# Outset of a two-block transformer kernel in column halves, with three chunks of the modulation loaded and summed elsewhere

## The chip, the cores and the metric

The kernel runs on one NeuronCore of a Trainium2 chip. The metric is the device time of one execution in microseconds (us). TensorE, VectorE, ScalarE, GpSimdE and SyncE are called PE, DVE, ACT, POOL and SP, as the profile does.

## The reference

One sequence of 512 tokens with 1024 features goes through two blocks. Only the first branch of the first block is touched here.

```python
cond = jax.nn.silu(c)
mod = cond @ w_ada[l] + b_ada[l]                     # 1024 -> 9 x 1024
sh1, sc1, gt1, sh2, sc2, gt2, sh3, sc3, gt3 = split(mod, 9)
u = rmsnorm(h, g_norm_ffn1) * (1 + sc1) + sh1
h = h + 0.5 * gt1 * swiglu(u, w_ffn1_in, w_ffn1_out) # 1024 -> 2 x 2816 -> 1024
...                                                  # token mixing, second feed-forward network,
                                                     # second block with two mixture-of-experts layers
```

## The kernel before

Activations lie feature-major: eight tiles k of 128 features by 512 tokens. A weight chunk is 1 MB, 128 partitions by 2048 numbers. Most matrix products are made of float32 numbers split in two: ACT copies a chunk or tile to a rounded high part (`weights_high`, L845; `tile_high`, L848), DVE subtracts to get the low part (`weights_low`, L1361; `tile_low`, L1367), and PE runs three matmuls of 128x512 for each tile (`passes`, L2193). A product over eight tiles is 24 matmuls.

**Stream.** SP loads all chunks of the first block in one fixed order (`stream_a`, issued at L600) into a ring of six slots (`slot_a`; slot n % 6 at the outset). Before each load it waits for the semaphore value that frees the slot; a load that waits holds all later ones back. The order at the outset is two chunks of the modulation matrix `w_ada`, x, six more chunks of `w_ada`, the two chunks of the first pair of the feed-forward network, three later chunks of `w_ada`, the second pair, two of `w_ada`, and so on. The first eight chunks (`ADA_FIRST`) hold scale and shift of the first norm, 256 rows by 1024 columns each (rows of 4 KB in memory); all other weight chunks of this stage are 1024 rows by 256 columns (1 KB). Chunks of the output matrix have 512 columns (2 KB).

**Outset.** PE multiplies the first two chunks by silu(c) (`ada_rows`, L2135), transposes x (L2178), takes two more chunks, spreads the reciprocal roots over the partitions (`rstd`, L2160), sums the scale (`ada_sums`, L2145), takes four chunks for the shift and sums it (L2145). ACT squares x (L829), evicts the eight transposed tiles to H (`evac`, L823) and then computes the root (L882, L886). DVE makes the reciprocals and a diagonal (`roots`, L1395, L1397), copies the scale rows (L1617), multiplies H by gain and reciprocal root (`normed`, L1631) and, when the shift is there, makes low parts of the tiles (L1638) while ACT makes high parts (L902). Only then does PE begin the first pair.

**Pairs.** The first projection of the network runs in 11 pairs, c = 0 to 10; a pair is four products, which = 0 or 1 (the silu side, `ffn_a`, and the other, `ffn_b`) for s = 0 or 1, into banks 2s + which. The first product starts the next as soon as DVE has multiplied the two results of a bank pair (`tile`, L1428, which signals `ffn_g`). In the gaps DVE adds up later chunks of `w_ada` weighted by silu(c) (`ada`, L1322 to L1335, one call for each chunk): three in pair 0, two in pairs 1 to 9, three in pair 10.

**Output projection.** `outproj` takes twelve chunks; chunk q needs the low part of its weights and, one by one, the low parts of its four tiles. DVE makes them in `out_low`, in this order for each q: whatever `idle` holds for q, then the chunk's low part, then four tiles:

```python
if q in idle:
    idle[q]()
...
if q:
    weights_low(split_at[name] + q)
    ...
            tile_low(m, pair, out_slot(name, q) + k - k0, rhs(k))
```

Before, `idle` holds `angles` for q = 2 and `modulation` for q = 4. The first four tiles of chunk 0 are made ahead, in pair 10.

Of the kernel before, what the change touches and what calls it, by code (L numbers as in the profile page):

```python
# [7 lines left out]
F32 = mybir.dt.float32  # L8
# [7 lines left out]
P = 128  # L16
# [113 lines left out]
def build(nc, A, out):  # L130
    with ExitStack() as ctx:
# [247 lines left out]
        def ffn_at(i, c):  # L379

            if i:
                return first["ffn1"] + 2 * c + (LATE_HERE if c else 0)
            return first["ffn0"] + (0 if c == 0 else 5 + 4 * (c - 1))

        def ada_of(c):

            a = ADA_FIRST + (0 if c == 0 else 3 + 2 * (c - 1))
            return list(range(a, a + (3 if c in (0, 10) else 2)))
# [14 lines left out]
        ada_first = tuple(range(ADA_FIRST))  # L403
# [58 lines left out]
        def slot_a(n):  # L462

            if n < first["mix"]:
                return n % RING
# [33 lines left out]
        for name, which, ns in [  # L499
                ("ffn0", "a", [ffn_at(0, c) + w for c in range(FT // 2) for w in range(2)]),  # L500
                ("ffn0_out", "a", range(first["ffn0_out"], first["ffn0_out"] + 12)),
# [314 lines left out]
        def _(act):  # L816
# [60 lines left out]
            def norm(i, shift, split=False):  # L877

                if i == 0:
                    act.wait_ge(sem("pool_step"), 4)  # L880
                    st.wait()
                A_(small[:, 56:57], epsc[:, 0:1], ACT.Sqrt)  # L882
                if i:
                    squares(i, range(4, KT))
                    act.wait_ge(sem("sumsq"), i)
# [4 lines left out]
                if i == 0:  # L890
                    act.wait_ge(sem("ada_mm"), 8)
                    act.wait_ge(sem("ada_mod"), 4)
                    for h in range(2):
                        evac(AROW[:, h], bank[4 + h][:], "ada_row")
                    weights_high(0)
                    act.wait_ge(sem("ada_mod"), ADA_FIRST)
                for k in range(KT):
                    if i == 0 and k == 2:
                        weights_high(1)
# [8 lines left out]
                if i == 1:  # L908
                    act.wait_ge(sem("u"), KT)
                    tile_high(UM[0][:, KT - 1], U[:, KT - 1])  # L910

            def ffn(i):
# [11 lines left out]
                weights_high(s0 + 3)  # L924
                with act.Fori(0, 3) as it:
# [185 lines left out]


            norm(0, lambda k: mod[:, k:k + 1], True)
            act.wait_ge(sem("side_tp"), 1)
            evac(LROW[0:64], bank[7][0:64, 64:64 + P], "side_out")
# [182 lines left out]
        def _(dve):  # L1298
# [122 lines left out]
            def ffn(i):  # L1421
# [8 lines left out]
                def some_ada(c, it, which):  # L1430

                    for m in which:
                        a = ada_of(c)[m]
                        now = a if it is None else it * 6 + a
                        ada(ffn_at(0, c) + 2 + m, now, a, 0 if it is None else it * 32)
# [6 lines left out]

                def pair(c, it, s_next):


                    n = 3 if c in (0, 10) else 2
# [21 lines left out]
                def modulation():  # L1468
                    if i:
# [15 lines left out]
                        {4: modulation} if i else {2: angles, 4: modulation}, staged=True)  # L1485
# [125 lines left out]
            nc.vector.tensor_copy(CZ[:, :, 0:1], csil[:].unsqueeze(2)).then_inc(sem("ada_cz"), 1)  # L1611

            def vector(v):
                if v == 0:
                    dve.wait_ge(sem("ada_mm"), 4)
                    for h in range(2):
                        nc.vector.tensor_copy(AROW[:, h], bank[4 + h][:]).then_inc(sem("ada_row"), 1)  # L1617
                dve.wait_ge(sem("ada_sum"), v + 1)
                c = KT * (1 - v)
                TTn(mod[:, c:c + KT], bank[7][:, 16 * v:16 * v + KT], par[:, PC["b_ada"] + c:PC["b_ada"] + c + KT], ALU.add)\  # L1620
                    .then_inc(sem("ada_mod"), 4)

            dve.wait_ge(sem("keep"), 16)
            roots(0)
            vector(0)
            dve.wait_ge(sem("ada_mod"), 4)
            modulated_gains(0)
            dve.wait_ge(sem("rstd"), 1)
            st.wait()
            for k in range(KT):  # L1630
                STT(out=U[:, k], in0=H[:, k], scalar=gains[:, k:k + 1], in1=bank[6][:],  # L1631
                    op0=ALU.mult, op1=ALU.mult).then_inc(sem("normed"), 1)
            vector(1)
            weights_low(0)
            dve.wait_ge(sem("ada_mod"), ADA_FIRST)
            for k in range(KT):
# [3 lines left out]
            weights_low(1)  # L1640
# [473 lines left out]
        def _(pe):  # L2114
# [11 lines left out]
            def ada_rows(a):  # L2126

                landed(pe, "a", ada_first[a])
                if a == 4:
                    pe.wait_ge(sem("ada_row"), 2)  # L2130
                w = chunk("a", ada_first[a])
                for half in range(2):
                    for k in range(2):
                        at = 32 * ((2 * half + 2 * a + k) % 4)
                        x = mm(bank[4 + half][at:at + 32, :], CZ[:, 2 * (a % 4) + k], w[:, k, 512 * half:512 * half + 512],  # L2135
                               start=(a % 4 < 2), stop=(a % 4 > 1))
                x.then_inc(sem("ada_mm"), 1)

            def ada_sums(v):

                for half in range(2):
                    pe.wait_ge(sem("ada_row"), 2 * v + half + 1)
                    for q in range(4):
                        c = 16 * v + 4 * half + q
                        x = mm(bank[7][:, c:c + 1], AROW[:, half, P * q:P * q + P], ones[:, 0:1], start=True, stop=True)  # L2145
                x.then_inc(sem("ada_sum"), 1)
# [22 lines left out]
            pe.wait_ge(sem("ada_cz"), 1)  # L2169
            ada_rows(0)  # L2170
            ada_rows(1)
            pe.wait_ge(sem("x_in"), 16)
# [10 lines left out]
            tp(bank[7][0:64, 64:64 + P], par[:, PC["ln1_g"]:PC["ln1_g"] + 64], ident).then_inc(sem("side_tp"), 1)  # L2183
            ada_sums(0)
            for a in range(4, ADA_FIRST):
                ada_rows(a)
# [9 lines left out]

            def ffn(i):
                a, b, g, base, s0 = sem("ffn_a"), sem("ffn_b"), sem("ffn_g"), FT * i, split_at[f"ffn{i}"]

                def pair(c, r, it):  # L2200

                    for s in range(2):
# [3 lines left out]
                        if s == 0 and it is None and r == 0 and i:  # L2206
                            pe.wait_ge(sem("w_low"), s0 + 2)
                        if it is None and r == s == 0:
                            tiles = [(which, k) for which in range(2) for k in range(KT)]
                            for which, k in sorted(tiles, key=lambda v: v[1]) if i else tiles:  # L2210
                                if i == 0 and k == 0:
                                    pe.wait_ge(sem("w_low"), s0 + which + 1)
# [14 lines left out]
                pair(0, 0, None)  # L2227
# [617 lines left out]
```

## Time and profile before

| | us |
|---|---|
| median of three runs (lowest, highest) | 2662.53 (2661.29, 2663.78) |
| profiled execution | 2662.51 |
| its span in the trace | 2660.5 |
| PE busy in the span | 2420.2 |

The trace starts with the first instruction. Each row of a timeline gives its start and its length in us, engine, line, operation, what it writes and reads, its shape and the number of instructions in the row; in brackets stands the idle time of the engine before it and what ended that.

### The profile page before, as it was taken

The page shows a single profiled execution, that of the slowest core. Times are in us where ns is not written, and L with a number is a line of the kernel's source. Part 1 is how long each engine was busy: PE and PEld are TensorE (multiplying, and loading weights), DVE is VectorE, ACT ScalarE, POOL GpSimd, SP SyncE. Part 2 cuts the span into 40 slices and gives each one's busy share as a digit, 9 for nine tenths or more (in the row PEclk, how much of TensorE's full clock was granted, in tenths as well). Part 3 has the DMA queues.
Part 4 walks back from the last instruction along what each step waited for, and adds up shares of the span by engine and source line. Part 5 has one row for each costly group of instructions (what it writes and reads, how often), then busy time and mean ns, then how long its engine had stood idle before and what let it go on. Part 6 is the DMA issues. An engine that isn't in the chain of part 4 may idle for free.

```text
span 2660.5 us, 38185 instructions
## 1 busy us (share of the span) xinstructions
PE 2420.2 (91%) x14539; PEld 1778.2 (67%) x14540; DVE 1353.0 (51%) x2767; ACT 860.4 (32%) x1484; POOL 215.5 (8%) x168
## 2 busy tenths in 40 slices
PE   6999999999999999999987887889989988888787
PEld 4888888877678888788754444547755865544454
DVE  5766645443552244543753444336955574344445
ACT  4222335565232223322322111124367341221122
POOL 1000003000000000000011111110036001111110
PEclk9999999999999999999999898899999999899899
DMA  8666422212333233221499999995220359999987
GB/s 287 213 196 196 166 87 86 67 48 80 131 110 102 100 103 102 96 95 64 180 386 422 422 422 422 422 401 196 80 95 19 149 196 422 422 422 422 422 339 306
DMA packets 201771, 591.62 MB, mean 222 GB/s; under 512 B 10512, under 2 KB 126432, under 8 KB 152784
## 3 DMA queue, kind: packets, MB, share of 16 engines
q1 hardware_dynamic: 198496, 575.47, 56.2%
q0 software_dynamic: 2896, 14.47, 1.7%
q8 instruction: 61, 1.00, 0.2%
q10 hardware_dynamic: 288, 0.43, 0.1%
q14 instruction: 30, 0.25, 0.0%
HBM read 588.17 MB, written 7.41 MB: 224 GB/s over the span
## 4 chain that ended last, share of the span: by engine, by line
PE 68%; DMA 21%; DVE 4%; ACT 3%; issue 2%; SPq 1%; POOL 1%; DVEq 0%; ACTq 0%; POOLq 0%
PE bank L2193 42%; DMA arena<-in_exp_w 19%; PE bank L2566 7%; PE bank L2287 4%; PE bank L2589 1%; SPq L611 1%; PE bank L2454 1%; PE bank L2607 1%; PE bank L2801 1%; PE bank L2377 1%; DVE ring_low L1361 1%; DMA ring<-in_exp_w 1%; PE bank L2535 1%; PE bank L2770 1%; PE bank L2536 1%
## 5 line engine op out<-in xcount | busy, mean ns | idle before, releaser
L2193 PE MATMUL bank<-parts 128*128 128x512 f32 x2560 | 795.4, 392 | 10.1 <-DVE parts L1638 4.3
L2193 PEld LDWEIGHTS bank<-parts 128*128 128x128 f32 x2560 | 482.1, 189 | 111.7 <-issue 6.5
L2193 PE MATMUL bank<-parts,ring_low 128*128 128x512 f32 x1280 | 500.3, 391 | 0.0
L2566 PE MATMUL bank<-ring,arena 128*32 128x256 f32 x2112 | 301.8, 445 | 84.6 <-DMA arena<-in_exp_w 84.4
L1361 DVE TENSOR_TENSOR ring_low<-ring,parts 128x2048 fp32r<-128x2048 f32 x109 | 245.1, 2252 | 177.8 <-ACT parts L845 168.6
L2566 PE MATMUL bank<-arena 128*32 128x256 f32 x2112 | 302.0, 445 | 33.2 <-issue 24.8
L845 ACT ACTIVATE parts<-ring 128x2048 fp32r<-128x2048 f32 x109 | 204.5, 1879 | 222.4 <-DMA ring<-in_w_ffn_in 114.4
L2193 PEld LDWEIGHTS bank<-parts,ring_low 128*128 128x128 f32 x1280 | 241.6, 189 | 51.1
L772 POOL COPY arena<-U 128x2048 f32<-128x2048 f32 x60 | 112.6, 1908 | 1756.0 <-PE bank L2566 1038.4
L2566 PEld LDWEIGHTS bank<-ring,arena 128*32 128x32 f32 x2112 | 141.6, 123 | 156.7 <-issue 132.6
L2566 PEld LDWEIGHTS bank<-arena 128*32 128x32 f32 x2112 | 144.5, 123 | 82.1 <-issue 50.0
L2193 PE MATMUL bank<-ring_low 128*128 128x512 f32 x576 | 194.1, 396 | 1.8 <-ACT arena L1157 1.8
L1077 ACT ACTIVATE arena<-bank 128x128 f32<-128x128 f32 x66 | 18.3, 278 | 537.3 <-PE bank L2566 537.3
L2607 PE MATMUL bank<-parts 128*128 128x512 f32 x496 | 129.8, 403 | 27.7 <-DVE parts L1924 26.8
L1919 DVE TENSOR_TENSOR arena<-bank,arena 128x128 f32<-128x128 f32 x66 | 19.2, 291 | 256.6 <-ACT arena L1077 256.6
L1940 DVE TENSOR_TENSOR H<-bank,H 128x512 f32<-128x512 f32 x232 | 143.8, 683 | 6.5 <-PE bank L2607 6.5
L2607 PEld LDWEIGHTS bank<-parts 128*128 128x128 f32 x496 | 87.2, 188 | 84.9 <-DVE parts L1924 40.2
L823 ACT ACTIVATE arena<-bank 128x512 f32<-128x512 f32 (+2 forms) x171 | 73.0, 467 | 209.4 <-PE bank L2536 95.4
L848 ACT ACTIVATE parts<-arena 128x512 fp32r<-128x512 f32 x128 | 71.4, 621 | 195.6 <-PE bank L2193 129.5
L1367 DVE TENSOR_TENSOR parts<-arena,parts 128x512 fp32r<-128x512 f32 x128 | 80.8, 687 | 105.5 <-ACT parts L848 105.2
L2193 PEld LDWEIGHTS bank<-ring_low 128*128 128x128 f32 x576 | 108.3, 188 | 31.0 <-issue 5.4
L2287 PE MATMUL bank<-parts 128*128 128x512 f32 x384 | 122.0, 395 | 3.9 <-DVE parts L1367 3.1
(380 smaller groups left out, 3584.1 us busy)
## 6 DMA issues: line engine op xcount, KB each, us to landing
ring<-in_exp_w SPq DMA_DIRECT2D x188, 1024.0 KB, 19.7
arena<-in_exp_w SPq DMA_DIRECT2D x132, 1024.0 KB, 18.6
U<-in_exp_w SPq DMA_DIRECT2D x60, 1024.0 KB, 23.1
ring<-in_w_ffn_in SPq DMA_DIRECT2D x44, 1024.0 KB, 5.6
ring<-in_w_ada SPq DMA_DIRECT2D x36, 1024.0 KB, 5.2
ring<-in_w_ffn_out SPq DMA_DIRECT2D x20, 1024.0 KB, 5.0
ring<-in_w_in SPq DMA_DIRECT2D x18, 1024.0 KB, 5.0
ring<-in_conv_w_in SPq DMA_DIRECT2D x12, 1024.0 KB, 5.1
```

Of the source, the lines that this page charges most:

```text
L611: sp.dma_start(dst, rows_of(layer, j, e)).then_inc(sem(f"w_e{3 * i + j}"), 16)
L772: pool.tensor_copy(W13[0][:, j], AHEAD[:, j]).then_inc(sem(f"w_e{j}"), 16)
L823: A_(dst, src, ACT.Copy).then_inc(sem(s), 1)
L845: A_(buf, ring[:, slots[which][n], 0:nk * cols], ACT.Copy).then_inc(sem("w_high"), 1)
L848: A_(dst, src, ACT.Copy).then_inc(sem("t_high"), 1)
L1361: TTn(ring_low[:, n, 0:nk * cols], ring[:, n, 0:nk * cols], buf.bitcast(F32), ALU.subtract)\
L1367: TTn(pair[1][:, at], src, pair[0][:, at].bitcast(F32), ALU.subtract).then_inc(sem("t_low"), 1)
L1940: x = TTn(H_, bank[sum_bank(t, h)][:], H_, ALU.add)
L2193: i = mm(o, a[:, cols[0], cols[1]], b, start=first_ and n == 0, stop=last_ and n == 2)
L2287: last = mm(bank[4 * half + t][:], a[:, at, P * t:P * t + P], b[:, k - 4 * c, :], start=(k == m == 0), stop=(k == kts - 1 and m == 2))
L2566: x = mm(bank[p][lanes_at:lanes_at + LANES, 0:2 * P].rearrange("p (w n) -> p w n", w=2), XW[:, k, LANES * (2 * p + e):LANES * (2 * p + e) ...
L2607: x = mm(bank[at][:], OHT[:, P * t:P * t + P], part[:, h], start=(j == 0), stop=(j == 1))
```

## The change

The outset works in column halves. The first eight chunks of `w_ada` become four rows of tiles by 512 columns (2 KB rows), ordered scale half 0, shift half 0, scale half 1, shift half 1; only four of them lie ahead of the first pair's weights, the other four behind. The slots of the first 15 loads are listed by hand. DVE, not ACT, evicts the transposed x to H. When four tiles of the normed input are done, PE multiplies them with the half chunks (`first_pair`), and between products makes the modulation of the other half. Pair 0 keeps one late chunk for DVE after its two tiles; two chunks move from it to the output projection, loaded as its third and fourth load and added up by DVE at q = 1. The transpose of the layer-norm parameters and its eviction move behind pair 0.

```diff
-            return first["ffn0"] + (0 if c == 0 else 5 + 4 * (c - 1))
+            return first["ffn0"] + (0 if c == 0 else 6 if c == 1 else 3 + 4 * c)
...
+                    if name == "ffn0_out" and n == 3:
+                        ada_chunks(2)
...
-                    stream_a.append((flat(A["w_ada"], 2 * (a % 4), 2, D * (1 - a // 4), D), 2, D, "ada_mm", a + 1))
+                    stream_a.append((flat(A["w_ada"], 4 * (a % 2), 4, D * (1 - a // 2 % 2) + 512 * (a // 4), 512), 4, 512,
+                                     "ada_mm", a + 1))
...
-        ada_chunks(ADA_FIRST)
+        ada_chunks(4)
...
-                    ada_chunks(3 if c in (0, 10) else 2)
+                    ada_chunks({0: 4, 1: 3, 10: 3}.get(c, 2))
...
+            if n < ffn_at(0, 2):
+                return (5, 0, 3, 4, 1, 2, 5, 0, 3, 4, 5, 0, 3, 1, 2)[n]
...
-            for k in range(KT):
-                act.wait_ge(sem("x_tp"), k + 1)
-                evac(H[:, k], bank[k % 4][:], "x_h")
...
+            def first_norm():
...
+                row(1)
+                first_high(0, 0)
+                act.wait_ge(sem("ada_mod"), 4)
+                tile(0)
+                tile(1)
+                first_high(1, 0)
+                tile(2)
+                tile(3)
+                first_high(0, 1)
+                first_high(1, 1)
+                row(2)
+                row(3)
+                act.wait_ge(sem("ada_mod"), ADA_FIRST)
+                for k in range(4, KT):
+                    tile(k)
...
+                def two_ada():
+
+                    for m in range(2):
+                        ada(first["ffn0_out"] + 2 + m, ADA_FFN - 2 + m, ADA_FFN - 2 + m)
...
+                    if i == 0 and c == 0:
+                        for s in s_next:
+                            weights_low(s)
+                        tile(0, 0)
+                        tile(1, 1)
+                        some_ada(0, None, range(1))
+                        return
...
-                        {4: modulation} if i else {2: angles, 4: modulation}, staged=True)
+                        {4: modulation} if i else {1: two_ada, 2: angles, 4: modulation}, staged=True)
...
+            dve.wait_ge(sem("ada_mm"), 2)
+            nc.vector.tensor_copy(AROW[:, 0], bank[4][:]).then_inc(sem("ada_row"), 1)
+            vector(0)
+            for k in range(KT):
+                dve.wait_ge(sem("x_tp"), k + 1)
+                nc.vector.tensor_copy(H[:, k], bank[k % 4][:]).then_inc(sem("x_h"), 1)
+                if k == 6:
+                    dve.wait_ge(sem("keep"), 16)
+                    roots(0)
+            dve.wait_ge(sem("x_h"), KT)
+            dve.wait_ge(sem("rstd"), 1)
+            normed(0)
+            vector(1)
+            first_low(0, 0)
+            rest_of(0)
+            normed(1)
+            rest_of(1)
+            normed(2)
+            first_low(1, 0)
+            rest_of(2)
+            normed(3)
+            rest_of(3)
+            first_low(0, 1)
+            first_low(1, 1)
+            vector(2)
+            for k in range(4, KT):
+                normed(k)
+            vector(3)
+            for k in range(4, KT):
+                rest_of(k)
...
+            def first_pair():
...
+                pe.wait_ge(sem("opening"), 2)
+                for k in range(4):
+                    pe.wait_ge(sem("t_low"), tiles_at["ffn0"] + k + 1)
+                    for s in range(2):
+                        product(0, s, k)
+                ada_rows(4)
+                ada_rows(5)
+                pe.wait_ge(sem("opening"), 3)
+                for k in range(4):
+                    product(1, 0, k)
+                    if k == 1:
+                        ada_sums(2)
+                ada_rows(6)
+                ada_rows(7)
+                for k in range(4):
+                    product(1, 1, k)
+                    if k == 1:
+                        ada_sums(3)
+                pe.wait_ge(sem("w_low"), 2)
+                for which in range(2):
+                    for k in range(4, KT):
+                        pe.wait_ge(sem("t_low"), tiles_at["ffn0"] + k + 1)
+                        for s in range(2):
+                            x = product(which, s, k)
+                            if k == KT - 1:
+                                x.then_inc(sem(("ffn_a", "ffn_b")[which]), 1)
```

## Rows read from the trace of the kernel before

**Rows 1.** The chain that ended last, 110 to 420 us: start, length, what, count.

```profile
109.93 195.52 PE bank L2193 x861
```

**Rows 2.** Waits of PE, 40 to 420 us: total us, times, longest.

```profile
PE bank L2193 <- DVE ring_low L1361: 0.7, 1, 0.7
```

**Rows 3.** Timeline of PE at the outset: start, length, line, shape, count [idle before].

```profile
16.71 3.67 PE L2178 MATMUL bank<-keep,arena 128*128 128x128 f32 x16 [3.19 <-DMA arena<-in_x]
21.49 2.11 PE L2178 MATMUL bank<-keep,arena 128*128 128x128 f32 x16 [1.11 <-ACT H L823]
...
30.26 3.64 PE L2135 MATMUL bank<-ring,arena 128*32 128x512 f32 x32
34.63 1.95 PE L2145 MATMUL bank<-ones,arena 128*128 128x1 f32 x16 [0.73 <-ACT arena L823]
40.92 1.19 PE L2193 MATMUL bank<-parts 128*128 128x512 f32 x2 [4.34 <-DVE parts L1638]
```

**Rows 4.** Timeline of ACT at the outset, and one half chunk later.

```profile
20.87 3.98 ACT L823 ACTIVATE H<-bank 128x512 f32<-128x512 f32 x8
...
26.26 0.28 ACT L886 ACTIVATE small<-small,epsc 128x4 f32<-128x4 f32 x1
...
40.72 3.77 ACT L902 ACTIVATE parts<-U,mod 128x512 fp32r<-128x512 f32 x6
...
318.99 1.05 ACT L845 ACTIVATE parts<-ring 128x1024 fp32r<-128x1024 f32 x1
```

**Rows 5.** Timeline of DVE at the outset, and one half chunk later.

```profile
27.65 1.28 DVE L1617 COPY arena<-bank 128x512 f32<-128x512 f32 x2
...
30.93 5.35 DVE L1631 SCALAR_TENSOR_TENSOR U<-H,gains,bank 128x512 f32<-128x512 f32 x8
...
37.81 2.29 DVE L1361 TENSOR_TENSOR ring_low<-ring,parts 128x2048 fp32r<-128x2048 f32 x1 [0.96 <-ACT parts L845]
...
320.06 1.23 DVE L1361 TENSOR_TENSOR ring_low<-ring,parts 128x1024 fp32r<-128x1024 f32 x1
```

**Rows 6.** Busy time by stretch: engines in turn, then clock, DMA share, GB/s.

```profile
10.00:20.00 10.00, 5.22 (x24) 3.47 (x24) 0.00 (x0) 3.31 (x7) 0.00 (x0) 1.00 1.02 414
30.00:40.00 10.00, 5.85 (x51) 3.04 (x51) 8.04 (x12) 5.21 (x6) 0.00 (x0) 0.89 1.08 352
285.00:290.00 5.00, 5.00 (x23) 3.99 (x22) 4.79 (x12) 3.32 (x5) 0.00 (x0) 1.00 1.01 379
40.92:44.66 3.74, 3.74 (x9) 2.97 (x10) 3.72 (x6) 3.73 (x7) 0.00 (x0) 0.50 1.10 347
```

**Rows 7.** Timeline of SP, the loads that the end of pair 0 frees.

```profile
64.75 1.00 SPq L600 DMA_DIRECT2D ring<-in_w_ada  x2
```

**Rows 8.** Timeline of DVE from pair 10 into the output projection.

```profile
274.48 2.29 DVE L1361 TENSOR_TENSOR ring_low<-ring,parts 128x2048 fp32r<-128x2048 f32 x1 [7.34 <-ACT parts L845]
...
279.69 0.61 DVE L1322 TENSOR_SCALAR arena<-ring,csil 128x256 f32<-128x256 f32 x2
...
289.24 0.68 DVE L1428 TENSOR_TENSOR arena<-bank,arena 128x512 f32<-128x512 f32 x1
...
292.04 2.49 DVE L1367 TENSOR_TENSOR parts<-arena,parts 128x512 fp32r<-128x512 f32 x4
...
303.19 2.49 DVE L1367 TENSOR_TENSOR parts<-arena,parts 128x512 fp32r<-128x512 f32 x4
```

**Rows 9.** Timeline of ACT, the tiles that wait for PE's first output chunk.

```profile
294.57 2.19 ACT L848 ACTIVATE parts<-arena 128x512 fp32r<-128x512 f32 x4 [4.05 <-PE bank L2193]
```

**Rows 10.** The page's DMA issues: KB each, median us from issue to landing.

```profile
ring<-in_w_ada SPq DMA_DIRECT2D x36, 1024.0 KB, 5.2
```

**Rows 11.** Timeline of PE, a later wait.

```profile
532.62 2.10 PE L2394 MATMUL bank<-arena 64*128 64x512 f32 x4 [2.13 <-ACT arena L1153]
```

**Rows 12.** Busy time of PE by stretch, then its clock, after two waits.

```profile
532.78:536.17 3.39, 3.39 (x14) 0.50 0.03 7
...
1508.99:1515.79 6.80, 5.85 (x56) 0.50 1.02 424
```

More of the change, by code:

```diff
@@ L402, in build @@
         first["ada"] = 0
-        ada_first = tuple(range(ADA_FIRST))
+        ada_first = tuple(a if a < 4 else a + 2 for a in range(ADA_FIRST))
         def ada_chunks(n):
@@ L500, in build @@
                 ("ffn0", "a", [ffn_at(0, c) + w for c in range(FT // 2) for w in range(2)]),
[L501 removed]
+                ("ffn0_out", "a", [first["ffn0_out"] + q + (2 if q > 1 else 0) for q in range(12)]),
                 ("mix", "a", [mix_at[c] for c in (0, 1, 2, 3, 4, 5, 6, 8, 9)]),
@@ L910, in norm, with first_high, row, tile @@
                     tile_high(UM[0][:, KT - 1], U[:, KT - 1])
+            def first_high(i, part):
+                which, n = splits[i]
+                landed(act, which, n)
+                C = slice(CHUNK // 2 * part, CHUNK // 2 * part + CHUNK // 2)
+                made = A_(high(i)[0][:, C], ring[:, slots[which][n], C], ACT.Copy)
+                if part == 0:
+                    st.did(made)
+                else:
+                    made.then_inc(sem("w_high"), 1)
+            def first_norm():
+                act.wait_ge(sem("pool_step"), 4)
+                st.wait()
+                A_(small[:, 56:57], epsc[:, 0:1], ACT.Sqrt)
+                A_(small[:, 48:52], small[:, 60:64], ACT.Sqrt, scale=1.0 / D, bias=epsc[:, 0:1]).then_inc(sem("root"), 1)
+                def row(g):
+                    act.wait_ge(sem("ada_mm"), 2 * g + 2)
+                    if g >= 2:
+                        act.wait_ge(sem("ada_sum"), g - 1)
+                    evac(AROW[:, g % 2], bank[4 + g % 2][:], "ada_row")
+                def tile(k):
+                    act.wait_ge(sem("normed"), k + 1)
+                    A_(UP[0][:, k], U[:, k], ACT.Identity, bias=mod[:, k:k + 1]).then_inc(sem("t_high"), 1)
+                row(1)
[13 more added lines that the diff above has]
+                    tile(k)
             def ffn(i):
@@ L1623, in _, with vector @@
[L1623 to L1630, printed above, removed]
+            nc.vector.tensor_copy(CZ[:, :, 0:1], csil[:].unsqueeze(2)).then_inc(sem("opening"), 1)
+            def vector(g):
+                dve.wait_ge(sem("ada_sum"), g + 1)
+                c = KT * (1 - g % 2) + 4 * (g // 2)
+                TTn(mod[:, c:c + 4], bank[7][:, 4 * g:4 * g + 4], par[:, PC["b_ada"] + c:PC["b_ada"] + c + 4], ALU.add)\
+                    .then_inc(sem("ada_mod"), 2)
+                dve.wait_ge(sem("ada_mod"), 2 * g + 2)
+                if g % 2 == 0:
+                    C = slice(2 * g, 2 * g + 4)
+                    seq(STT(out=gains[:, C], in0=mod[:, c:c + 4], scalar=1.0, in1=par[:, PC["g_ffn1"] + 2 * g:PC["g_ffn1"] + 2 * g + 4],
+                            op0=ALU.add, op1=ALU.mult))
@@ L1631, in _, with first_low, normed @@
+            def first_low(i, part):
+                dve.wait_ge(*((sem("act_step"), TT + i + 1), (sem("w_high"), i + 1))[part])
+                n = slots["a"][splits[i][1]]
+                C = slice(CHUNK // 2 * part, CHUNK // 2 * part + CHUNK // 2)
+                TTn(ring_low[:, n, C], ring[:, n, C], high(i)[0][:, C].bitcast(F32), ALU.subtract)\
+                    .then_inc(sem(("opening", "w_low")[part]), 1)
+            def normed(k):
                 STT(out=U[:, k], in0=H[:, k], scalar=gains[:, k:k + 1], in1=bank[6][:],
@@ L1632, in _, with rest_of @@
                     op0=ALU.mult, op1=ALU.mult).then_inc(sem("normed"), 1)
[L1633 to L1636, printed above, removed]
+            def rest_of(k):
                 dve.wait_ge(sem("t_high"), tiles_at["ffn0"] + k + 1)
@@ L2205, in pair @@
                             pe.wait_ge(g, c * 2 + (base + s - 1))
-                        if s == 0 and it is None and r == 0 and i:
+                        if s == 0 and it is None and r == 0:
                             pe.wait_ge(sem("w_low"), s0 + 2)
                         if it is None and r == s == 0:
[L2209 to L2212, printed above, removed]
+                            for which, k in [(which, k) for k in range(KT) for which in range(2)]:
                                 pe.wait_ge(sem("t_low"), tiles_at[f"ffn{i}"] + k + 1)
```

85 lines of the change are left out of this document (33 added, 52 removed).

## The prediction

> **What bounds the kernel now.** I read the chain that ended last first. From 110 to 305 us it is one row of matmuls, 861 in 195.52 us, 0.227 us each [rows 1]: in the first stage PE never waits, so time counts only where PE is idle, runs at the lower clock or gets extra work. The waits of PE confirm it: between 40 and 420 us there are two waits for the first projection's operands, 4.34 us ahead of the first pair [rows 3] and 0.7 us in the third pair [rows 2]. Then the timelines: of PE, ACT and DVE at the outset, to see what the first pair waits for; and of DVE where the output projection begins, because the change puts work there. Last the stretches with the clock. Two places matter:
>
> The outset. x is there at 16.7 us, but the first pair starts at 40.92 [rows 3], and the loads that its end frees go out at 64.75 [rows 7]; so pair 0 ends at 64.75. Of these 23.8 us, 96 matmuls at 0.227 are 21.8. Most of the rest is the clock: from 40.92 to 44.66 it is at 0.50, 1.2 GHz, after an engine that had waited 4.34 us, and 9 matmuls start where 16.5 would have [rows 6], a loss of 7.5 x 0.227 = 1.7 us.
>
> The start of the output projection. PE ends its first chunk at 294.5 (ACT's tiles that wait for this start at 294.57 [rows 9]). The second chunk needs a tile that DVE begins at 292.04; four take 2.49 [rows 8], so the first is there at 292.7. DVE is 1.8 us ahead, no more, and it has no idle time from 276.7 on: it comes out of two late chunks (279.69 to 289.24, 9.55 us for both [rows 8]).
>
> **The change, part by part.** Durations come from the profiled execution, 2662.51 us, which is the median of the three runs to 0.02; so the sum is made against 2662.5.
>
> 1. Loads ahead of x. The two chunks now have rows of 2 KB, not 4. Loads ran at 414 GB/s where rows were 4 KB and 379 where output chunks with 2 KB rows dominate [rows 6]: 1.049 MB takes 2.77 in place of 2.53 us, so x lands 0.5 us later, at 17.2. The Trainium skill's page "DMA: Bandwidth & Descriptors" (Why small descriptors are slow) tells of a fixed overhead of about 3 cycles for a packet beside one cycle for 32 bytes, which would make 2 KB rows 2.3% dearer than 4 KB rows: 0.1 us for both chunks, and a total 0.4 us lower. The rows are nearer to this case, and I keep them. Behind x come two chunks (2.77 each), then the pair's weights at 352 GB/s [rows 6], 2.98 each: 25.7 and 28.7, where the first of them used to land at 35.9. The other four chunks follow by 40, ahead of their use.
>
> 2. Eviction of x moves from ACT to DVE. ACT needs 3.98 us for eight and could not start before 20.87, because it squares x [rows 4]; a DVE copy of this size costs 1.28 for two [rows 5], 0.6 in sequence. The skill's page "VectorE: DVE Perf Modes" (its first table, Memory placement) has ScalarE closer to PSUM, which speaks against the move; the rows agree in sign, 0.1 us a tile, and by that alone 0.8 us would be lost. But DVE is free from the first transposed tile on. Transposes take 3.67 + 2.11 us without the 1.11 us in which PE waited for an eviction [rows 3]: 17.2 to 23.0. The root no longer stands behind 3.98 us of evictions: 26.26 - 3.98 + 0.5 = 22.8 [rows 4]. From there to the end of DVE's root work took 1.39 us (26.26 to 27.65 [rows 4, 5]): 24.2; the last eviction ends at 24.8. PE's two chunks at 0.91 (3.64 for four) and the spreading of the roots, eight instructions at 0.13 (2.11 for 16) [rows 3], end at 25.9. The first normed tile starts there, where it started at 30.93 [rows 5].
>
> 3. The ladder of four tiles. On DVE: eight tile operations at 0.67 (5.35 for eight), two half weights at 1.23 [rows 5], 0.2 for the shift, and two waits for ACT's high part, 0.63 [rows 4] and hand-over 0.1 each, the other two being covered by the half weights. Sum 5.4 + 2.5 + 0.2 + 1.5 = 9.6, so the fourth tile's low part is there at 35.5, and with 0.15 to PE at 35.7. Halving costs 2 x 1.23 - 2.29 = 0.17 us a chunk on DVE, hidden for the later halves. PE's two products for a tile are 1.36 us, less than the ladder's 2.4 a tile.
>
> 4. PE from there: the last tile, 1.36, to 37.1; then four chunks of the other half (3.64), two groups of sums (1.95) [rows 3] and 24 matmuls (5.45): 48.1. Their evictions by ACT lie beside the products that stand behind them. The last sum ends 1.36 earlier, at 46.8; shift, high and low part of tile 4 take 0.2 + 0.7 + 0.75 + 0.1, to 48.5: PE idles 0.4. Then 48 matmuls, 10.9, to 59.4. Both results of s = 0 now end almost together, so pair 1 waits for one DVE multiply: 59.7. The wait stands behind DVE's two `weights_low` of pair 1, which end at about 59. **Gain 64.75 - 59.7 = 5.0 us.**
>
> 5. The clock on this way. PE idles some 2 us before the ladder and is sparse on it; a wait of 2.13 us [rows 11] was followed by 3.39 us at 0.50 [rows 12], so I expect a low stretch here. A tile costs about 2.5 us then, as much as the ladder. Bounds: nothing, or a stretch like the longest shown, 5.85 us of work at 0.50 [rows 12], wholly on the dense part: 5.85 x 7.5/16.5 = 2.7. I take 0.4, since PE's work begins 8 us before the dense part does.
>
> 6. Pair 0 keeps one late chunk in place of three, behind its tiles, so DVE is not late in pairs 1 and 2; the 0.7 us wait [rows 2] goes. **Gain 0.7.** The parameters' transpose and its eviction moved behind pair 0 cost PE one short instruction. SP's loads for the late chunks of pair 1 now wait for pair 0 and hold pair 2's weights back, as a wait there did before; these are needed 20 us later, so I cost that at nothing; without the cover it would be one landing, 5.2 us [rows 10].
>
> 7. Two late chunks at q = 1. They stand on DVE ahead of the second output chunk's low part and its four tiles. Everything behind moves by 9.55: the first tile is there at 292.7 + 9.55 = 302.3 (on the clock of before), where PE is done at 294.5. **PE idles 7.8 us.** Their loads do not make it later: they go out when the last product of the projection ends, 48 x 0.23 = 11 us before 294.5, land in 5.2 us [rows 10], at 288.6, and DVE is not free until 289.8. Next late is the third chunk: its first tile was begun at 303.19 [rows 8], 11.15 us behind the second chunk's; PE needs 10.9 for a chunk, so nothing more is lost.
>
> 8. The clock behind that wait. A wait of this length is followed by a low stretch, of 3.39 to 5.85 us of work [rows 12]: 1.5 to 2.7 us; at least nothing. I take 2.0, near what pair 0 paid (1.7) [rows 6].
>
> Sum: -5.0 - 0.7 + 0.4 + 7.8 + 2.0 = +4.5, **2667.0 us**. With the bounds of 5 and 8: 2662.5 - 5.7 + 7.8 = 2664.6 to 2662.5 - 5.7 + 2.7 + 7.8 + 2.7 = 2670.0.
>
> **The rivals.**
>
> A, not slower: DVE reaches q = 1 earlier, so the two chunks are covered. For: it idles 7.34 us ahead of 274.48 [rows 8], and pair 10 could start sooner. Against: that idle time is a wait for ACT and so for the load of the first output chunk, which stands in the same order behind the same three late chunks and is freed by the same pair 9. It decides if DVE is 7.8 us earlier against PE; if all the idle time went, 0.5 us of wait is left, no low clock: 2662.5 - 5.3 + 0.5 = 2657.7.
>
> B, slower: the outset's low clock falls on the dense part after 37 us, not on the ladder. For: PE is sparse until then, and pair 0 was at 0.50 for its first 3.74 us [rows 6]. Against: at 0.50 the ladder itself keeps PE busy. It decides if the clock is still low at 37: 2.3 us more, 2669.3; with the longer low stretch in the output projection 2670.0.
>
> C, the change does not do what it says: first products at 28 us still wait on something I miss on ACT (a row eviction behind its half chunks) and pair 0 ends at 62, a gain of 2.7 in place of 5: 2669.3. Nothing in the rows shows it.
>
> **How the numbers follow.** Forecast 0.57, A 0.13, B 0.17, C 0.13. About 0.2%, 5.3 us, is what a measurement of this kernel can tell from no change, so faster means under 2657.2, slower over 2667.8. A lies just inside; with half its spread beyond, and a remainder from the forecast's mechanism being wrong altogether, faster 0.09. The forecast's own range, 2664.6 to 2670, has about a quarter of its chance above 2667.8 (0.14); with B and C nearly whole, slower is 0.41, same 0.50. Range: A's 0.13 and 0.05 above are left out: 2661.5 to 2671.
>
> **What would show it.** In the changed profile: the first matmul of the pair at about 29 us, DVE's first normed tile at 26, pair 0 ending near 59.5, no wait near 90 us; in the output projection a wait of PE near 8 us for DVE's tile low parts (L1367's successor), its weights' low part directly behind ten operations of two late chunks, and the clock at 0.50 behind it. Wrong would be a wait there under 3 us (then A), or pair 0 ending after 61 (then B or C, told apart by the clock after 37 us).

## The result and the profile after

| | before | after |
|---|---|---|
| median of 15 runs each, us | 2662.53 | 2667.43 |
| lowest to highest, us | 2658.68 to 2667.40 | 2664.58 to 2670.25 |
| profiled execution, us | 2662.51 | 2666.85 |
| its span, us | 2660.5 | 2665.0 |

The ratio after to before is 1.0017, with a 95% interval of 1.0010 to 1.0024: 4.9 us more, and 4.3 more between the two profiled executions. That is inside the 0.2% within which the prediction speaks of no change, but the interval leaves out 1: the kernel became a little slower, although its first pair ends 4.8 us earlier. Where the gain went is to be read in four places. All medians here and below are of fast executions; the slow ones, all over 3000 us (one of the kernel before in the later runs, one of e4_act_evicts, two of e7_busy_outset), are left out.

**PE at the outset and in the output projection**, timeline of the kernel after: start, length, line, shape, count [idle before, and what ended it].

```profile
16.71 5.65 PE L2258 MATMUL bank<-keep,arena 128*128 128x128 f32 x32 [0.52 <-DMA arena<-in_x]
28.43 1.19 PE L2269 MATMUL bank<-parts 128*128 128x512 f32 x2 [2.34 <-DVE parts L1689]
36.88 1.92 PE L2214 MATMUL bank<-ring,arena 128*32 128x512 f32 x16
48.91 0.70 PE L2269 MATMUL bank<-parts 128*128 128x512 f32 x2 [0.53 <-DVE parts L1689]
59.92 0.27 PE L2305 MATMUL bank<-keep,par 128*64 128x128 f32 x1
60.34 0.73 PE L2269 MATMUL bank<-parts 128*128 128x512 f32 x2
...
297.19 1.19 PE L2269 MATMUL bank<-parts 128*128 128x512 f32 x2 [7.74 <-DVE parts L1405]
```

L2269 is the product line (L2193 in [rows 3]), L1689 the low part of a tile at the outset (L1638), L1405 the low part of a tile of the output projection (L1367). x is there at 16.71, to the hundredth as in [rows 3]. The first product stands at 28.43 where it stood at 40.92, but it is the start of a ladder that DVE paces; the dense work begins at 36.88. Pair 0 ends at 59.92 and pair 1 starts at 60.34, where pair 0 ended and pair 1 began at 64.75. From there the chain that ended last is again one row of matmuls:

```profile
60.34 196.16 PE bank L2269 x864
```

864 matmuls in 196.16 us are 0.227 each, the step of [rows 1]: a lead won ahead of this row is carried through it unchanged. The first chunk of the output projection ends at 297.19 - 7.74 = 289.45, against 294.5 before: 5.05 us ahead. Then PE waits 7.74 us, and the lead is gone.

**The waits of PE** from 40 to 420 us in the kernel after: in total, times, longest.

```profile
PE bank L2269 <- DVE parts L1405: 7.7, 1, 7.7
PE bank L2463 <- ACT U L897: 1.7, 1, 1.7
PE bank L2239 <- DVE diag L1435: 0.9, 1, 0.9
PE bank L2269 <- DVE parts L1689: 0.5, 1, 0.5
```

The 0.7 us of [rows 2] in the third pair is no longer there; the 7.7 is new. **DVE around it**, timeline:

```profile
269.28 2.29 DVE L1399 TENSOR_TENSOR ring_low<-ring,parts 128x2048 fp32r<-128x2048 f32 x1 [7.23 <-ACT parts L851]
...
284.63 0.61 DVE L1360 TENSOR_SCALAR arena<-ring,csil 128x256 f32<-128x256 f32 x2
289.49 0.62 DVE L1360 TENSOR_SCALAR arena<-ring,csil 128x256 f32<-128x256 f32 x2
294.16 2.28 DVE L1399 TENSOR_TENSOR ring_low<-ring,parts 128x2048 fp32r<-128x2048 f32 x1
296.36 2.49 DVE L1405 TENSOR_TENSOR parts<-arena,parts 128x512 fp32r<-128x512 f32 x4
```

L1360 is the first operation of a late chunk (L1322 in [rows 8]), L1399 the low part of a weight chunk (L1361). The two late chunks that q = 1 got stand from 284.63 to 294.16, 9.5 us, ahead of the low part of the second chunk's weights. PE runs out of operands at 289.45, when DVE is between the first of them and the second. **The clock behind the wait**, busy time by stretch (PE, weight loads, DVE, ACT, POOL, each with its instructions; then granted clock, DMA share, GB/s):

```profile
293.80:297.15 3.35, 0.00 (x0) 0.00 (x0) 3.33 (x4) 1.72 (x1) 0.00 (x0) 0.50 0.05 18
297.19:300.60 3.41, 3.41 (x8) 2.73 (x9) 3.31 (x7) 0.00 (x0) 0.00 (x0) 0.50 0.00 0
300.65:310.00 9.35, 9.35 (x49) 7.43 (x47) 9.10 (x14) 0.00 (x1) 0.00 (x0) 1.00 0.01 2
```

The granted clock falls to 0.50 (1.2 GHz) while PE waits, and stays there for the first 3.41 us of work: 8 matmuls start in it, where the step of 0.227 us would make it 15, so 7 x 0.227 = 1.6 us are lost. The sum from these rows is -5.05 + 7.74 + 1.6 = +4.3 us, which is the difference of the profiled executions.

### The profile page after: what moved, and what is told of

The parts are those of the page before. It is cut to its first block, busy times and chain, and to the rows that moved or that the text cites. A ratio compares the mean times of both kernels' runs of the same rounds, so it can differ in the third digit from the quotient of the medians.

```text
span 2665.0 us, 38207 instructions
## 1 busy us (share of the span) xinstructions
PE 2427.1 (91%) x14539; PEld 1780.4 (67%) x14540; DVE 1358.2 (51%) x2779; ACT 857.9 (32%) x1479; POOL 215.5 (8%) x168
## 4 chain that ended last, share of the span: by engine, by line
PE 66%; DMA 22%; DVE 5%; issue 2%; ACT 2%; SPq 1%; POOL 1%; DVEq 0%; POOLq 0%
PE bank L2269 41%; DMA arena<-in_exp_w 19%; PE bank L2676 7%; PE bank L2397 4%; DMA ring<-in_exp_w 2%; PE bank L2699 1%; SPq L621 1%; PE bank L2564 1%; PE bank L2911 1%; DVE ring_low L1399 1%; PE bank L2487 1%; PE bank L2880 1%; PE bank L2717 1%; PE bank L2645 1%; PE bank L2646 1%
## 5 line engine op out<-in xcount | busy, mean ns | idle before, releaser
L2269 PE MATMUL bank<-parts 128*128 128x512 f32 x2560 | 798.2, 393 | 15.8 <-DVE parts L1405 7.7
L2269 PEld LDWEIGHTS bank<-parts 128*128 128x128 f32 x2560 | 482.9, 189 | 120.3 <-issue 9.6
L2269 PE MATMUL bank<-parts,ring_low 128*128 128x512 f32 x1280 | 501.3, 392 | 0.0
L1399 DVE TENSOR_TENSOR ring_low<-ring,parts 128x2048 fp32r<-128x2048 f32 x107 | 240.5, 2251 | 181.0 <-ACT parts L851 172.3
L2269 PEld LDWEIGHTS bank<-parts,ring_low 128*128 128x128 f32 x1280 | 242.5, 189 | 51.1
L2269 PE MATMUL bank<-ring_low 128*128 128x512 f32 x576 | 194.1, 396 | 1.8 <-ACT arena L1195 1.8
L833 ACT ACTIVATE arena<-bank 128x512 f32<-128x512 f32 (+3 forms) x172 | 73.7, 468 | 215.4 <-PE bank L2646 95.4
L1405 DVE TENSOR_TENSOR parts<-arena,parts 128x512 fp32r<-128x512 f32 x128 | 80.7, 686 | 104.1 <-ACT parts L854 103.8
L2269 PEld LDWEIGHTS bank<-ring_low 128*128 128x128 f32 x576 | 108.4, 188 | 30.9 <-issue 5.4
```

The source lines that it names most:

```text
L833: A_(dst, src, ACT.Copy).then_inc(sem(s), 1)
L1399: TTn(ring_low[:, n, 0:nk * cols], ring[:, n, 0:nk * cols], buf.bitcast(F32), ALU.subtract)\
L1405: TTn(pair[1][:, at], src, pair[0][:, at].bitcast(F32), ALU.subtract).then_inc(sem("t_low"), 1)
L2269: i = mm(o, a[:, cols[0], cols[1]], b, start=first_ and n == 0, stop=last_ and n == 2)
```

## Experiments

The theory: the wait at q = 1 is DVE's 9.5 us of two late chunks set against the lead of 1.8 us that DVE has there, and costs 7.7 us and the clock behind it; it has nothing to do with the new outset. The rivals: the wait came with the outset (PE reaches q = 1 sooner); the loads are late; or the outset gained less than the timeline suggests and something later gives it back.

Each ratio below is taken against executions of the kernel before that ran beside that kernel (median 2662.57 us beside e1, e2, e3 and e5, 2662.89 beside e4, e6 and e7). The intervals are about as wide as the effects, and most that one would compare overlap. The profiled executions are sharper. The chain that ended last holds, in all nine kernels, a row of 18 matmuls, 4.21 us long, near the end of the output projection. The last column counts to it from the start of pair 1 (with the old outset, from the loads that the end of pair 0 frees), so it leaves out the outset and all that stands behind the projection.

| kernel | pair 1 begins, us | row of 18 begins, us | between, us |
|---|---|---|---|
| before | 64.75 | 399.24 | 334.49 |
| after | 60.34 | 403.75 | 343.41 |
| e1_late_q4 | 60.19 | 394.00 | 333.81 |
| e2_out_alone | 64.36 | 407.08 | 342.72 |
| e3_one_q1 | 60.13 | 398.58 | 338.45 |
| e4_act_evicts | 64.30 | 407.88 | 343.58 |
| e5_kept_busy | 60.85 | 402.68 | 341.83 |
| e6_three_pair0 | 60.09 | 396.58 | 336.49 |
| e7_busy_outset | 60.82 | 394.64 | 333.82 |

**e1_late_q4: the two late chunks at another place.** The kernel after, with the work of the two chunks put three output chunks later. Their loads stay where they are, and so does all of the outset.

```diff
-                        {4: modulation} if i else {1: two_ada, 2: angles, 4: modulation}, staged=True)
+                        {4: modulation} if i else {2: angles, 4: two_ada, 5: modulation}, staged=True)
...
-                        if a1 and half == 0 and c == 2:
+                        if a1 and half == 0 and c == (4 if name == "ffn0_out" else 2):
```

> The changed kernel with its two late chunks added up at q = 4 of the output projection in place of q = 1; the fold of the sums on PE moves to the fifth output chunk and the modulation to q = 5. Loads and their order stay. Theory (the loss of the change is DVE's order at q = 1): DVE has some 9 us to spare before the fifth chunk's low parts are due, so the 7.7 us wait of PE and the low clock behind it (3.4 us of work at 1.2 GHz, 1.6 us lost) go: 2667.4 - 9.3 = 2658.1, and the wait at the second output chunk is gone from the profile. Rival (two more loads ahead of the third output chunk, or the ring's new slots, hold PE back wherever the sums stand): a wait of 3 us or more remains in the output projection, 2663 or more.

Measured: 2658.26 us, 0.9983 of before (0.9974 to 0.9992). The waits of its PE from 40 to 420 us, and a stretch with the first of the two chunks, which now stand from 304.85 to 314.39 us on DVE:

```profile
PE bank L2463 <- ACT U L897: 1.7, 1, 1.7
PE bank L2239 <- DVE diag L1435: 1.0, 1, 1.0
PE bank L2269 <- DVE parts L1689: 0.5, 1, 0.5
```

```profile
300.00:310.00 10.00, 10.00 (x45) 8.28 (x45) 9.68 (x19) 4.01 (x5) 0.00 (x0) 1.00 0.24 57
```

The wait is gone and no other has come in its place; DVE is busy for 9.68 of 10 us and PE for 10.00 of 10 beside it, at full clock. The difference to the kernel after is 9.2 us by the medians and 343.41 - 333.81 = 9.6 in the table, against 7.7 + 1.6 = 9.3 from the rows. This version is ahead of both kernels. It does not answer the question of the loads, since they have 20 us more to land here; the kernel after does: its DVE begins the multiply ahead of the chunks at 284.04, the first chunk at 284.63 and the second at 289.49, with no idle time before either, so it did not wait for the loads.

**e2_out_alone: the output projection's part alone.** The outset of before, with only the late chunks moved: pair 0 keeps one, two are loaded behind the first chunks of the output projection and added up at q = 1.

```diff
-            a = ADA_FIRST + (0 if c == 0 else 3 + 2 * (c - 1))
-            return list(range(a, a + (3 if c in (0, 10) else 2)))
+            a = ADA_FIRST + (0 if c == 0 else 1 + 2 * (c - 1))
+            return list(range(a, a + {0: 1, 10: 3}.get(c, 2)))
...
+                    if name == "ffn0_out" and n == 3:
+                        ada_chunks(2)
...
-                        {4: modulation} if i else {2: angles, 4: modulation}, staged=True)
+                        {4: modulation} if i else {1: two_ada, 2: angles, 4: modulation}, staged=True)
```

> The kernel before with only the late chunks moved: one in pair 0, two at q = 1 of the output projection with their loads third and fourth there. The outset is that of before. Theory: the same 7.8 us wait and low clock (1.6 to 2.0) as in the changed kernel, less the 0.7 us wait of the third pair, which goes: 2662.5 + 8.9 = 2671.4. Rival (the wait arises because the changed outset shifts DVE against PE): no wait or a short one, 2662 to 2665.

Measured: 2670.94 us, 1.0032 of before (1.0019 to 1.0044). The first two rows of its waits of PE, from 20 to 420 us (its L1369 is the low part of a tile of the output projection, its L1645 that of a tile at the outset), and the matmul behind the first of these waits:

```profile
PE bank L2200 <- DVE parts L1369: 7.7, 1, 7.7
PE bank L2200 <- DVE parts L1645: 4.5, 1, 4.5
```

```profile
300.80 1.19 PE L2200 MATMUL bank<-parts 128*128 128x512 f32 x2 [7.67 <-DVE parts L1369]
```

The same 7.7 us with PE 3.7 us later (it runs out of work at 300.80 - 7.67 = 293.13, against 289.45), and the outset's old wait (4.34 in [rows 3], 4.5 here) is still paid. So the wait belongs to the place q = 1: DVE's lead is a lead over PE, and an earlier outset moves both. It also prices the two halves of the change: the moved chunks cost 2670.9 - 2662.6 = 8.4 us by the medians and 342.72 - 334.49 = 8.2 in the table (7.7 + 1.6 less the 0.7 of the third pair would be 8.6). The new outset brings 2670.9 - 2667.4 = 3.5 by the medians, but the intervals of this kernel and of the kernel after overlap (1.0019 to 1.0024); in the profiles pair 1 begins 64.36 - 60.34 = 4.0 us earlier.

**e3_one_q1: one late chunk at q = 1, the other at q = 4.** The size of the cause is halved; `two_ada` takes the number of the chunk.

```diff
-                        {4: modulation} if i else {1: two_ada, 2: angles, 4: modulation}, staged=True)
+                        {4: modulation} if i else {1: lambda: two_ada(0), 2: angles, 4: lambda: two_ada(1), 5: modulation}, staged=True)
```

> Half the dose: one late chunk at q = 1, the other at q = 4. Theory: DVE is 1.8 us ahead there and a chunk costs 4.8, so PE waits 3.0 us, and the clock still falls: 2658.1 + 3.0 + 1.6 = 2662.7, 2661.1 if so short a wait leaves the clock alone. Rival (the wait is set by the landing of the two loads, not by DVE's work): the wait stays near 5 to 8 us, 2665 or more.

Measured: 2662.41 us, 0.9994 of before (0.9985 to 1.0003). Its wait at q = 1, from the waits of PE, and two stretches, the wait and what follows it; then the first and the last matmuls that start in the second stretch:

```profile
PE bank L2268 <- DVE parts L1405: 2.8, 1, 2.8
```

```profile
289.30:292.00 2.70, 0.00 (x0) 0.01 (x1) 2.70 (x3) 2.70 (x4) 0.00 (x0) 1.00 1.00 366
293.15:296.55 3.40, 3.40 (x10) 2.65 (x9) 3.23 (x7) 1.57 (x1) 0.00 (x0) 0.50 0.15 57
```

```profile
293.33 0.63 PE L2268 MATMUL bank<-parts,ring_low 128*128 128x512 f32 x1
...
296.31 0.74 PE L2268 MATMUL bank<-parts 128*128 128x512 f32 x2
```

One chunk is 4.75 us of DVE (half of 9.5); less the lead of 1.8 that leaves 3.0, and 2.8 is what PE waits. The lead is thus a fixed sum that is paid from once: one chunk costs 2.8, the second its whole length. The clock was still at 1.00 in this wait and is at 0.50 from 293.15. The stretch counts 10 matmuls, but two of them began before it: eight start in it, from 293.33 to 296.31, where 15 would, so 7 x 0.227 = 1.6 us are lost, as much as behind the wait of 7.74. Together that is 4.4 us; the table has 338.45 - 333.81 = 4.6 against e1_late_q4, and the medians 4.2, though these two intervals overlap (0.9985 to 0.9992). The profiled execution took 2658.30 us, no longer than that of e1_late_q4 (2658.31): it is behind at the row of 18 and makes this up later, where single executions differ by some microseconds for reasons that were not looked into.

**e5_kept_busy: the wait kept, the clock held.** The kernel after, with 31 matmuls on operands that are there into a free bank ahead of the second output chunk; their result is not used.

```diff
+                        if name == "ffn0_out" and half == 0 and c == 1:
+                            pe.wait_ge(sem("ffn_g"), FT - 1)
+                            for m in range(31):
+                                mm(bank[0][:], STAGE[0][:, (m + 1) % 4, 0:P], STAGE[0][:, m % 4], start=True, stop=True)
```

> The changed kernel with 31 matmuls of 128x512 more on PE ahead of the second output chunk, into a bank that is free then; their result is not used. At 0.227 us they fill 7.0 of the 7.7 us in which PE waits. Theory: the wait itself is DVE's and stays, but the clock stays at 2.4 GHz, so 1.6 us come back: 2665.8. Rival (the low clock there costs nothing, since DVE hands over tile by tile): 2667.4; or the matmuls cost what they take: 2674.

Measured: 2664.96 us, 1.0009 of before (1.0000 to 1.0018). The stretch behind the wait:

```profile
297.75:301.20 3.45, 3.45 (x15) 2.88 (x16) 3.33 (x7) 0.00 (x0) 0.00 (x0) 1.00 0.02 5
```

15 matmuls at 1.00, where the kernel after has 8 at 0.50 in a stretch of nearly the same length. So the low clock there does come from the idle PE, and its cost in the trace is about the 1.6 us worked out above. The time agrees in sign (2.5 us less than the kernel after), but the two intervals overlap from 1.0010 to 1.0018. The profiles show the effect: in the table this kernel is 343.41 - 341.83 = 1.6 us faster, with the wait for DVE still in it.

**e4_act_evicts: the eviction of x back on ACT.** The kernel after, with ACT doing the eight evictions behind its squares, as before.

```diff
+                for k in range(KT):
+                    act.wait_ge(sem("x_tp"), k + 1)
+                    evac(H[:, k], bank[k % 4][:], "x_h")
...
-            for k in range(KT):
-                dve.wait_ge(sem("x_tp"), k + 1)
-                nc.vector.tensor_copy(H[:, k], bank[k % 4][:]).then_inc(sem("x_h"), 1)
-                if k == 6:
-                    dve.wait_ge(sem("keep"), 16)
-                    roots(0)
+            dve.wait_ge(sem("keep"), 16)
+            roots(0)
```

> The changed kernel with the eviction of x back on ACT, behind its squares; the rest as changed. Theory (the ladder starts early because the root no longer waits for eight evictions on ACT): the root comes 4 us later, at 26.5, the spread roots at 28.6, the first normed tile at 28.6 where the changed kernel has 25.43; all behind moves by 3.2: 2667.4 + 3.2 = 2670.6. Rival (the ladder hangs on the loads of the half weights or on the scale, so the eviction's place is worth nothing): 2667.4.

Measured: 2670.56 us, 1.0026 of before (1.0015 to 1.0038). ACT's root and DVE's first normed tile, first in this kernel, then in the kernel after:

```profile
27.05 0.28 ACT L924 ACTIVATE small<-small,epsc 128x4 f32<-128x4 f32 x1
...
29.31 0.75 DVE L1687 SCALAR_TENSOR_TENSOR U<-H,gains,bank 128x512 f32<-128x512 f32 x1 [0.76 <-PE bank L2238]
```

```profile
22.45 0.28 ACT L921 ACTIVATE small<-small,epsc 128x4 f32<-128x4 f32 x1
...
25.43 0.75 DVE L1684 SCALAR_TENSOR_TENSOR U<-H,gains,bank 128x512 f32<-128x512 f32 x1 [0.86 <-PE bank L2239]
```

The normed tile is 3.9 us later. By the medians the kernel is 3.1 us slower than the kernel after, but these intervals overlap (1.0015 to 1.0024). The profiles are clear: pair 1 begins at 64.30 in place of 60.34, 4.0 us later, and only 0.06 us ahead of e2_out_alone and 0.45 of before, which have the whole old outset. So the gain of the outset hangs on this edit: with ACT evicting, the order in halves brings less than half a microsecond. The eviction alone, with the chunks whole, was not tried, so it is open whether the edit needs the halves.

**e6_three_pair0: the new outset alone.** The kernel after, with three late chunks behind the tiles of pair 0, as before, none at q = 1, and ring slots laid out for that.

```diff
-            a = ADA_FIRST + (0 if c == 0 else 1 + 2 * (c - 1))
-            return list(range(a, a + {0: 1, 10: 3}.get(c, 2)))
+            a = ADA_FIRST + (0 if c == 0 else 3 + 2 * (c - 1))
+            return list(range(a, a + {0: 3, 10: 3}.get(c, 2)))
...
-                        some_ada(0, None, range(1))
+                        some_ada(0, None, range(3))
...
-                        {4: modulation} if i else {1: two_ada, 2: angles, 4: modulation}, staged=True)
+                        {4: modulation} if i else {2: angles, 4: modulation}, staged=True)
```

> The new outset alone: three late chunks in pair 0 behind its tiles as before the change, none in the output projection; the ring's slots are laid out for that order. Theory: no wait and no low clock in the output projection, as with the chunks at q = 4 (2658.3), but DVE comes late into pair 2: three chunks end near 75 us, two more and two low parts of weights near 90, where PE wants them at 88: waits of 0.9 and 1.6 us there, 2660.8. Rival (pair 0 has room for them): 2658.3; or the waits go on from pair to pair: 2664 or more.

Measured: 2661.38 us, 0.9992 of before (0.9983 to 1.0001). Two waits in the timeline of its PE:

```profile
83.05 0.73 PE L2267 MATMUL bank<-parts 128*128 128x512 f32 x2 [0.89 <-DVE arena L1464]
...
89.97 0.73 PE L2267 MATMUL bank<-parts 128*128 128x512 f32 x2 [1.17 <-DVE ring_low L1397]
```

With three chunks DVE is late in the third pair, by 0.89 and 1.17 us where it was 0.7 before [rows 2]: PE comes earlier and the chunks do not shrink. The two make 2.1 of the 336.49 - 333.81 = 2.7 us by which this kernel stands behind e1_late_q4 in the table; the rest was not traced (the medians say 3.1, but their intervals overlap from 0.9983 to 0.9992). So the profiles speak for taking two chunks out of pair 0, and against the place they were put to.

**e7_busy_outset: what the low clock on the ladder costs.** e1_late_q4 with two unused float32 products, two instructions each in the trace, into a free bank ahead of the first pair.

```diff
+                for m in range(2):
+                    mm(bank[4][:], ones[:], xtok[:, m, 0:512], start=True, stop=True)
```

> The kernel with the late chunks at q = 4, and two more float32 matmuls of 128x512 on PE between the sums of the shift and the first pair, into a free bank; their result is not used. They fill most of the 2.4 us in which PE idles there. Theory (step 5 of the prediction: the low clock on the ladder costs next to nothing, since DVE's hand-over sets its pace): the low stretch shrinks or goes and the time stays within 0.4 us of 2658.3. Rival (the low clock there costs what its 6.8 us suggest): 1.5 to 3 us less, 2655.3 to 2656.8.

Measured: 2657.85 us, 0.9979 of before (0.9969 to 0.9988), against 2658.26 without them. The ladder in e1_late_q4, then in this kernel: the stretch, the first product and the chunks behind the ladder, and one of this kernel's waits on it:

```profile
27.30:34.10 6.80, 5.72 (x14) 4.55 (x15) 5.46 (x8) 2.91 (x4) 0.00 (x0) 0.50 1.05 387
...
28.38 1.19 PE L2269 MATMUL bank<-parts 128*128 128x512 f32 x2 [2.38 <-DVE parts L1689]
...
36.73 1.92 PE L2214 MATMUL bank<-ring,arena 128*32 128x512 f32 x16
```

```profile
26.50:37.30 10.80, 8.45 (x30) 4.89 (x29) 8.97 (x13) 5.74 (x7) 0.00 (x0) 1.00 1.05 385
...
29.02 0.70 PE L2269 MATMUL bank<-parts 128*128 128x512 f32 x2 [0.51 <-DVE parts L1689]
...
33.58 0.73 PE L2269 MATMUL bank<-parts 128*128 128x512 f32 x2 [0.80 <-DVE parts L1689]
...
37.38 1.92 PE L2214 MATMUL bank<-ring,arena 128*32 128x512 f32 x16
```

The clock is at 1.00 throughout, and nothing is gained: from the first product to the chunks are 36.73 - 28.38 = 8.35 us at the low clock and 37.38 - 29.02 = 8.36 at the full one. Where PE was slow it now waits for DVE. On this stretch, which DVE paces, the low clock costs next to nothing.

## Why the prediction was right, step by step

**Bound.** Right. [rows 1] and the chain of after have the same 0.227 us a matmul, and all that changed is in the waits ahead of and behind that row.

**Step 1, x later by 0.5 us: mis-sized.** x came at 16.71, as before; from 10 to 20 us the loads ran at 404 GB/s:

```profile
10.00:20.00 10.00, 7.09 (x32) 5.28 (x33) 2.83 (x6) 3.31 (x7) 0.00 (x0) 1.00 1.04 404
```

Only part of that stretch is a test: up to 16.7 us most of what moves is x, whose rows are 4 KB in both kernels. From 17 to 20 us the kernel before still loads 4 KB rows and the kernel after 2 KB rows alone (584 packets, 1.16 MB):

```profile
17.00:20.00 3.00, 3.00 (x16) 2.98 (x14) 0.00 (x0) 3.00 (x7) 0.00 (x0) 1.00 1.02 406
17.00:20.00 3.00, 3.00 (x16) 3.00 (x15) 1.82 (x3) 3.00 (x7) 0.00 (x0) 1.00 1.05 388
```

So 2 KB rows were 4.4% slower here, not 8.5% as by the 379 GB/s that I had taken from [rows 6]. That stretch has 2 KB rows too, but a load only begins in it; from 286 to 290 us it has 403 GB/s. The Trainium skill's page "DMA: Bandwidth & Descriptors" (Why small descriptors are slow) gave 2.3% by its fixed overhead for a packet. That is about half of the 4.4%, and still nearer than my row. By 4.4% the two chunks ahead of x would take 0.2 us longer; why none of that reached x is not shown.

**Steps 2 and 3, the eviction and the ladder.** The root stands at 22.45 (22.8 in the working) and the first normed tile at 25.43 (25.9): 0.35 and 0.47 us earlier, which is about step 1's half microsecond. The last low part of the ladder is there at 34.38 + 0.75 = 35.13 (35.5):

```profile
34.38 0.75 DVE L1689 SCALAR_TENSOR_TENSOR parts<-U,mod,parts 128x512 fp32r<-128x512 f32 x1 [0.79 <-ACT parts L931]
```

From 25.43 that is 9.7 us for the ladder, against 9.6. A DVE eviction took 0.64 us, an ACT one 0.50 (3.98 for eight [rows 4]):

```profile
20.42 2.56 DVE L1697 COPY H<-bank 128x512 f32<-128x512 f32 x4 [0.16 <-PE bank L2258]
```

The Trainium skill's page "VectorE: DVE Perf Modes" (Specifications, Memory placement) has ScalarE closer to PSUM, and for the single instruction the trace agrees in sign. e4_act_evicts shows that this doesn't decide here: with the dearer instructions on DVE the first normed tile came 3.9 us sooner.

**Step 4, the dense part: 0.7 us too short.** It began at 36.88 (37.1) and ended at 59.92 (59.4): 23.0 us instead of 22.3. The idle before tile 4 was 0.53 (0.4), and the 48 matmuls behind it took 59.92 - 48.91 = 11.0 (10.9). The largest part is the mixed stretch: four chunks of the other half, two groups of sums and 24 matmuls took 48.91 - 0.53 - 36.88 = 11.5 us, where the working had 3.64 + 1.95 + 5.45 = 11.04. By the starts in PE's timeline it is the matmuls that were too cheap: in four groups of six (the first from 38.73 to 40.22) they took 6.2 us, the chunks 3.7 and the sums 1.6. Behind pair 0 the parameters' transpose, "one short instruction" in step 6, and the hand-over take 0.42 (0.3 in the working). Gain 4.4 at the start of pair 1, against 5.0.

**Step 5, the clock at the outset.** Placed right: low on the ladder, full in the dense part.

```profile
27.55:34.37 6.82, 5.94 (x14) 4.77 (x15) 5.25 (x8) 3.13 (x5) 0.00 (x0) 0.50 1.05 386
34.40:48.40 14.00, 13.98 (x83) 8.69 (x82) 6.69 (x11) 4.26 (x6) 0.00 (x0) 1.00 0.95 322
```

I took 0.4 us for it; e7_busy_outset says about nothing.

**Step 6.** The 0.7 us wait is gone, as forecast. With the 4.4 of pair 0 it makes the 5.05 us that PE is ahead at the end of the first output chunk; the working had 5.3.

**Step 7, two chunks at q = 1.** The wait was 7.74 us (7.8). The third chunk brought no further wait, and the loads, issued when the projection's last product ended, were not what came last:

```profile
278.27 0.99 SPq L610 DMA_DIRECT2D ring<-in_w_ada  x2
```

e1_late_q4 to e3_one_q1 confirm the mechanism from three sides: elsewhere no wait, the same wait with the old outset, and 2.8 us for one chunk.

**Step 8, the clock behind it.** 1.6 us by the trace, 2.0 in the working, inside its bounds.

**The rivals.** A needed DVE to come to q = 1 earlier against PE; its idle time ahead of the output projection is 7.23 us (7.34 in [rows 8]) and moved with PE, so its lead stayed 1.8. B needed a low clock after 37 us; the row from 34.40 has 1.00. C needed the first product to wait for something unseen; it stands at 28.43, where the working had about 29.

So the sum held because its largest terms, 7.8 and 5.0, were each within 0.7. That the smaller errors nearly cancel is luck: up to 36.88 the working was 0.2 too slow, from there to pair 1 0.9 too fast, and the two clock terms were 0.4 each too dear.

## What to carry to other kernels

When work is taken off a critical stretch, look for a place where its engine's lead over the bound covers it, not for the place where its operands happen to land: the same 9.5 us of DVE cost 9.2 us at q = 1, where DVE is 1.8 us ahead, and nothing three chunks later. A wait of the engine that bounds is to be priced with the clock behind it (1.6 us behind 2.8, and 1.6 behind 7.7), while a low clock on a stretch that another engine paces may stand. And a dearer instruction on a free engine can be worth far more than a cheaper one on an engine that comes late: 0.14 us a tile lost, 4.0 us won at the start of pair 1.

## What I had not expected of the hardware

Two loads of 1 MB with 2 KB rows ahead of x instead of 4 KB rows left the arrival of x where it was, at 16.71 us. And a wait as short as 2.8 us, at the end of which the clock was still at 1.00, was followed by as long a stretch of work at 0.50 (eight matmuls in 3.40 us) as one of 7.7 us, in which it had fallen before the wait ended (eight in 3.41 us).
